# Hybrid encoder step on one core: order of the first loads, squares of the second tile on VectorE, order of the closings

## The reference, cut to what matters

```
h = x + W_out[concat(shortconv(xn), ssd(xn))],   xn = RMSNorm(x) * ln_mix_w,  xn @ W_in first
h = h + CrossAttn(RMSNorm(h), memory)            4 heads, 256 memory tokens
h = h + PEER(RMSNorm(h))                         8 heads x 16 experts per token out of 16384
y = RMSNorm(h) * final_norm_w
```

## Time and profile before

| | us |
|---|---|
| median of three runs | 1840.97 |
| their range | 1833.16 to 1843.06 |
| the profiled execution | 1838.45 |
| its span, first to last instruction | 1836.7 |
| TensorE, VectorE, GpSimd, ScalarE busy | 1689.9, 1225.0, 697.7, 369.2 |

### The profile page before, as it was taken

The page is one execution under the profiler, slowest core; times in us unless marked ns, Lnnn a source line. Parts: engine busy times, 40 slices in busy tenths (PEclk is TensorE's granted clock), DMA queues, the critical chain, the costliest instruction groups (busy, mean ns, idle before and its releaser), DMA issues. The chain is left out here.

```text
span 1836.7 us, 19834 instructions
## 1 busy us (share of the span) xinstructions
PE 1689.9 (92%) x7088; PEld 1256.1 (68%) x7088; DVE 1225.0 (67%) x2437; ACT 369.2 (20%) x912; POOL 697.7 (38%) x598
## 2 busy tenths in 40 slices
PE   6998999999777888898896999999999999999996
PEld 5887888877655677787785666666666666666542
DVE  1252111799688768898986999676656666656675
ACT  1031123111330244642660001101000000000101
POOL 0000000234124437731664555555444544534551
PEclk9999999999878999899898999999999999999998
DMA  5532444779336949995999999999999999999995
GB/s 168 180 110 99 153 138 138 240 249 349 101 134 204 379 167 367 338 329 184 361 346 415 409 409 410 409 407 410 406 409 410 397 410 409 396 409 405 377 409 221
DMA packets 238301, 563.10 MB, mean 307 GB/s; under 512 B 17068, under 2 KB 125276, under 8 KB 236156
## 3 DMA queue, kind: packets, MB, share of 16 engines
q0 software_dynamic: 82944, 302.03, 42.7%
q1 hardware_dynamic: 121512, 242.72, 36.1%
q10 hardware_dynamic: 33748, 17.10, 3.1%
HBM read 539.46 MB, written 21.66 MB: 306 GB/s over the span
## 5 line engine op out<-in xcount | busy, mean ns | idle before, releaser
L782 POOL DMA_INDIRECT M<-in_u_tab,IDX x288 | 331.3, 1150 | 736.5 <-DVE PEER L1742 358.0
L789 POOL DMA_INDIRECT M<-in_v_tab,IDX x288 | 362.8, 1260 | 369.2 <-DVE X L1763 299.3
L1093 PE MATMUL PSB<-XN,M 128*128 128x256 f32 x2048 | 469.0, 384 | 12.2 <-ACT M L1303 6.0
L1101 PE MATMUL PSB<-M,HST 128*128 128x512 f32 x1024 | 461.3, 596 | 10.4 <-DVE HST L1819 9.6
L1093 PEld LDWEIGHTS PSB<-XN,M 128*128 128x128 f32 x2048 | 393.5, 193 | 112.8 <-issue 53.2
L1742 DVE CUSTOM_DVE_ANT_0 M<-M,XN 128x1024 f32<-128x1024 f32 x288 | 351.8, 1223 | 146.7 <-DMA M<-in_u_tab,IDX 135.3
L1763 DVE SCALAR_TENSOR_TENSOR X<-M,PEER,X 128x1024 f32<-128x1024 f32 x256 | 328.1, 1282 | 101.4 <-DMA M<-in_v_tab,IDX 88.0
L831 PE MATMUL PSB<-M 128*128 128x256 f32 (+1 forms) x1408 | 333.4, 398 | 10.2 <-DVE M L1399 8.9
L1101 PEld LDWEIGHTS PSB<-M,HST 128*128 128x128 f32 x1024 | 194.8, 191 | 215.1 <-issue 198.5
L831 PEld LDWEIGHTS PSB<-M 128*128 128x128 f32 x1408 | 270.1, 193 | 66.4 <-DVE M L1399 9.8
L838 PE MATMUL PSB<-M 128*128 128x256 f32 (+1 forms) x1056 | 247.7, 395 | 2.5 <-DVE M L1399 1.6
(11 more groups left out here) (214 smaller groups left out, 1072.7 us busy)
## 6 DMA issues: line engine op xcount, KB each, us to landing
M<-in_u_blocks SPq DMA_DIRECT2D x128, 512.0 KB
M<-in_v_tab SPq DMA_DIRECT2D x128, 512.0 KB
M<-in_w_in SPq DMA_DIRECT2D x24, 1024.0 KB
M<-in_w_pq SPq DMA_DIRECT2D x16, 1024.0 KB
gate_spill<-M ACTq DMA_DIRECT2D x16, 1024.0 KB, 14.5
M<-gate_spill SPq DMA_DIRECT2D x16, 1024.0 KB, 11.1
M<-in_w_out SPq DMA_DIRECT2D x8, 1024.0 KB
M<-in_w_mq SPq DMA_DIRECT2D x8, 1024.0 KB
```

The costliest lines, as they stand in the source:

```text
L782: pool.indirect_dma_start(out=UA[:, s % RR, :], out_offset=None, in_=utab, in_offset=bass.IndirectOffsetOnAxis(ap=IDX[:, n:n + 1], axis=0) ...
L789: pool.indirect_dma_start(out=VA[:, s % RR, :], out_offset=None, in_=vtab, in_offset=bass.IndirectOffsetOnAxis(ap=IDX[:, n:n + 1], axis=0) ...
L1093: last = pe.matmul(PSB[:, 4 + b % 2, 0:2 * P], UBLK[:, b % SR, c, :], XN[:, 1:3, c * P:(c + 1) * P], start=(c == 0), stop=(c == DC - 1))
L1101: last = pe.matmul(PSB[:, 2 * t + hf, :], WR[:, b % WRING, t * P:(t + 1) * P], VBLK[:, b % SR, hf * 512:(hf + 1) * 512], start=(b == 0), s ...
```

## The change

At the start, SP loads tile 0, tile 1 and five of the nine small tables, and only then weight block 0, block 1, the state and block 2; ScalarE issues the other four small loads. VectorE sums the squares of tile 1 (`sq`), and ScalarE only takes the root of it; the list begins with `sq` of tile 1, `norm` of tile 0, `const`, `norm` of tile 1, and both turns. At the end, `fold` stands ahead of the last block's `vd`; then come both closings, the three roots in the order sample, tile 1, tile 2, and the three final scalings in that order. Closing tile 1 waits for the half of the last block that belongs to it.

```diff
+CLOSED = [4, 1, 2]
+SMALL_ROWS = [("ln_mix_w", ...), ("mem_norm_w", ...), ("ln_mem_w", ...), ("ssd_norm_w", ...), ("conv_a_w", ...),
+              ("conv_s_w", ...), ("conv_s_b", ...), ("cache_conv_a", ...), ("cache_conv_ssd", ...)]
@@ dense
     if g == 0:
-        s += [("const",)]
-        for t in TG[0]:
-            s += [("norm", 0, t), ("turn", 0, t)]
+        s += [("sq", 1), ("norm", 0, 0), ("const",), ("norm", 0, 1), ("turn", 0, 0), ("turn", 0, 1)]
@@ plan
+        if b == NBLK - 1:
+            out.append(("fold",))
         out.append(("vd", b))
...
-    for t in DENSE:
-        out += [("close", t), ("leave", t), ("final", t)]
-    return out + [("fold",), ("leave", NP), ("final", NP)]
+    out += [("close", t) for t in DENSE] + [("leave", t) for t in CLOSED]
+    return out + [("final", t) for t in CLOSED]
@@ SP
             sp.dma_start(X[:, 0, :], xp[0]).then_inc(x_in[0], 16)
+            sp.dma_start(X[:, 1, :], xp[1]).then_inc(x_in[1], 16)
+            for row in SMALL_ROWS[4:]:
+                load_small(sp, *row)
             load_block(sp, 0)
-            sp.dma_start(X[:, 1, :], xp[1]).then_inc(x_in[1], 16)
             load_block(sp, 1)
+            sp.dma_start(S0[:, :, :], a["state_ssd"]...).then_inc(state_in, 16)
             load_block(sp, 2)
@@ TensorE, vd
+                    if b == NBLK - 1 and t == 0:
+                        last.then_inc(first_closed, 1)
@@ ScalarE, norm
+                if (ph, t) == (0, 1):
+                    act.wait_ge(sq_done, 1)
+                    col = ROOTS.index(("norm", 0, 1))
+                    act.activation(SS[:, col:col + 1], SS[:, col:col + 1], ACT.Sqrt, bias=EPSC[:, :], scale=1.0 / D).then_inc(root_done, 1)
+                    return
@@ ScalarE, leave
-                if t in DENSE:
-                    act.wait_ge(closed, DENSE.index(t) + 1)
-                elif t < NP:
+                if t in CLOSED:
+                    act.wait_ge(closed, CLOSED.index(t) + 1)
+                else:
                     act.wait_ge(v_added, (step_of(t, PH - 1) + 1) * TOPK)
-                else:
-                    act.wait_ge(closed, 3)
@@ ScalarE, start
-            for name, r, pat in (... nine tables ...):
-                src = a[name].rearrange(pat, p=P)
-                act.dma_start(SMR[r:r + src.shape[0], :], src).then_inc(small_in, 16)
-            act.dma_start(S0[:, :, :], a["state_ssd"]...).then_inc(state_in, 16)
+            for row in SMALL_ROWS[:4]:
+                load_small(act, *row)
@@ VectorE
+            def sq(t):
+                col = ROOTS.index(("norm", 0, t))
+                dve.wait_ge(const_ok, 1)
+                dve.wait_ge(x_in[t], 16)
+                dve.tensor_tensor_reduce(XN[:, t, :], X[:, t, :], X[:, t, :], 1.0, 0.0, ALU.mult, ALU.add, SS[:, col:col + 1]).then_inc(sq_done, 1)
@@ VectorE, close
-                dve.wait_ge(vd_done, NBLK)
+                if t == DENSE[0]:
+                    dve.wait_ge(first_closed, 1)
+                else:
+                    dve.wait_ge(vd_done, NBLK)
```

More of the change, by code:

```diff
@@ L49 @@
 DENSE = [1, 2]
+CLOSED = [4, 1, 2]
+SMALL_ROWS = [("ln_mix_w", SM_MIX, "l (c p) -> (l c) p"), ("mem_norm_w", SM_MEMN, "l (c p) -> (l c) p"),
+              ("ln_mem_w", SM_LMEM, "l (c p) -> (l c) p"), ("ssd_norm_w", SM_SSD, "l (c p) -> (l c) p"),
+              ("conv_a_w", SM_CA, "l k (c p) -> (l k c) p"), ("conv_s_w", SM_CS, "l k (c p) -> (l k c) p"),
+              ("conv_s_b", SM_CB, "l (c p) -> (l c) p"), ("cache_conv_a", SM_HA, "l b k (c p) -> (l b k c) p"),
+              ("cache_conv_ssd", SM_HS, "l b k (c p) -> (l b k c) p")]
 def rows(t):
@@ L549, in build_program @@
         act_step, dve_step = sem("act_step"), sem("dve_step")
-        root_done = sem("root_done")
+        root_done, sq_done = sem("root_done"), sem("sq_done")
         xs_done = sem("xs_done")
@@ L567, in build_program @@
         gs_out, gr_in = [sem(f"gs_out{r}") for r in range(3)], [sem(f"gr_in{r}") for r in range(GRING)]
-        y_norm, y_out = sem("y_norm"), sem("y_out")
+        y_norm, y_out, first_closed = sem("y_norm"), sem("y_out"), sem("first_closed")
         def loc(t, gap=0):
@@ L618, in score_at, with load_small @@
             return [GAIN[:, 0:512], GAIN[:, 512:1024], EARLY[:, 0:512], EARLY[:, 512:1024]][b]
+        def load_small(eng, name, r, pat):
+            src = a[name].rearrange(pat, p=P)
+            eng.dma_start(SMR[r:r + src.shape[0], :], src).then_inc(small_in, 16)
         def load_block(sp, i):
@@ L632, in _ @@
             sp.dma_start(X[:, 0, :], xp[0]).then_inc(x_in[0], 16)
+            sp.dma_start(X[:, 1, :], xp[1]).then_inc(x_in[1], 16)
+            for row in SMALL_ROWS[4:]:
+                load_small(sp, *row)
             load_block(sp, 0)
-            sp.dma_start(X[:, 1, :], xp[1]).then_inc(x_in[1], 16)
             load_block(sp, 1)
+            sp.dma_start(S0[:, :, :], a["state_ssd"].rearrange("l b (x h) p n -> (h p) (l b x) n", h=2)).then_inc(state_in, 16)
             load_block(sp, 2)
@@ L1346, in leave @@
                 n = rows(t)
-                if t in DENSE:
-                    act.wait_ge(closed, DENSE.index(t) + 1)
-                elif t < NP:
+                if t in CLOSED:
+                    act.wait_ge(closed, CLOSED.index(t) + 1)
+                else:
                     act.wait_ge(v_added, (step_of(t, PH - 1) + 1) * TOPK)
-                else:
-                    act.wait_ge(closed, 3)
                 root_mean_square(("leave", t), XN[0:n, t, :], X[0:n, t, :], n, D)
[L1355 to L1359, removed]
-                src = a[name].rearrange(pat, p=P)
-                act.dma_start(SMR[r:r + src.shape[0], :], src).then_inc(small_in, 16)
-            act.dma_start(S0[:, :, :], a["state_ssd"].rearrange("l b (x h) p n -> (h p) (l b x) n", h=2)).then_inc(state_in, 16)
+            for row in SMALL_ROWS[:4]:
+                load_small(act, *row)
             act.wait_ge(const_ok, 1)
@@ L1833, in final @@
                 dve.scalar_tensor_tensor(out=x, in0=x, scalar=rs, in1=GAIN[0:n, :], op0=ALU.mult, op1=ALU.mult).then_inc(y_norm, 1)
-            does = {"const": const, "state": state, "norm": norm, "turn": turn, "memn": memn, "in": in_, "keep": keep, "ca": ca, "cs": cs, "dt": dt, "oc": oc,
+            does = {"sq": sq, "const": const, "state": state, "norm": norm, "turn": turn, "memn": memn, "in": in_, "keep": keep, "ca": ca, "cs": cs, "dt": dt, "oc": oc,
                     "kt": kt, "s1": s1, "s2": s2, "s3": s3, "s4": s4, "o": residual("o"), "a1": a1, "mo": residual("mo"),
```

## The result

The changed kernel takes 1821.8 us (median of 4 runs, 1818.53 to 1828.5) against 1841.04 (median of 4, 1833.16 to 1843.06). The ratio is 0.9911, 95% interval 0.9888 to 0.9935, which is 12 to 20.6 us less. I had said 1830.5 us and 10.5 us less, with a range down to 1825.5.

A forecast was written before the change was run, and what follows sets the result against it. It took the body as dense TensorE work, then saturated DMA transfer, with serial chains at both ends. Gains of 4.7 us at the start and 5.85 at the tail, 10.5 off 1840.97, gave 1830.5 us, range 1825.5 to 1838.

The forecast's parts named there:

- the size of the start: Before the first projection: starting at 13.3 instead of 18.03 us gains 4.7 us, with bounds of 2.0 and 5.8.
- tile 1's landing: Start loads: tile 1, issued second at about 1.27 us, lands at 6.4 us, with bounds 5.3 and 9.1.
- my second estimate: Tile 1's landing from the byte count plus the 1.1 to 1.4 us by which landings trail their bytes: 6.5 us.
- the first job: First sixteen matmuls of the projection: expected to take about 6.1 us again, as in the kernel before.
- TensorE reaches its full clock sooner: Rival at the first projection: nearly gapless transposes lift the clock, gaining up to 2.7 us more, 1827.8 us; chance 0.10.
- The tail: End of the kernel: fold before the last block and interleaved closings gain 5.85 us, with bounds 2.9 and 7.4.
- table load: ScalarE's activation table load in the closings: counted at 1.28 us, without the skill's 1.38 us drain.
- The larger last output: At the very end, a 512 KB tile goes out last instead of the 128 KB sample, giving back 0.65 us.
- The fold's wait: Before the last block: the last gather addition ends 3.0 us ahead of the fold, so TensorE waits for nothing.
- Start is lost on the way: Rival in the body: it absorbs what the start saves, leaving only the tail's gain, 1835.1 us; chance 0.16.
- slower, by the clock in the middle: Rival between 400 and 1000 us: 39 us more at half clock cost 19.5 us, giving 1850 us; chance 0.05.
- VectorE's squares cost nothing: Start: tile 0's scaling, queued behind tile 1's squares, goes at 7.8 instead of 6.3 us, without cost to the projection.

The follow-up runs named there:

- the change again: The changed kernel unaltered, run a second time in more rounds beside its halves; ratio 0.9924 to the kernel before.
- e6: Changed kernel with all nine small loads issued from ScalarE's queue; one run, within 1826.2 to 1829.8 us for four such kernels, beside 1841.2 before.
- e8: Changed kernel with tile 1's closing waiting for the whole last block; one run, within 1826.2 to 1829.8 us for four such kernels, beside 1841.2 before.
- the delayed one: Changed kernel with five idle repetitions of VectorE's sum of squares, 6.1 us, ahead of the real one; ratio 0.9952 to the kernel before.
- e12: Changed kernel without VectorE's squares, Sqrt table loaded before the fold, sample's last scaling on GpSimd, tile 2 scaled and sent in halves; ratio 0.9931 to before.
- third profile: Profile from the third set of runs of the unaltered changed kernel; that set's ratio was 0.9922 to the kernel before.
- start alone: Kernel before with only the change's start: loads, squares of tile 1 on VectorE, order of first steps; ratio 0.9952 to the kernel before.
- e5: Changed kernel with ScalarE squaring tile 1 instead of VectorE; one run, within 1826.2 to 1829.8 us for four such kernels, beside 1841.2 before.
- e7: Changed kernel with early fold but closings one after another, waiting for the whole block; one run, within 1826.2 to 1829.8 us for four such kernels.

## Why the prediction was wrong, and where it held

**What failed: the size of the start.** I had the projection start at 13.3 and gain 4.7 us; it starts at 12.47 and gains 5.6 by this row, 5.9 by the second copy, 6.7 in the mean of the profiles. Two terms of the sum were off. First, tile 1's landing, taken at 6.4, is 5.8 in the trace. The step from tile 0 to tile 1 was right: 1.35 us (4.41 to 5.76), where 524 KB at 385 GB/s had given 1.36. What was off was its start, since tile 0 itself lands at 0.81 + 3.6 = 4.41 and not at the 4.81 of the kernel before, and my second estimate: by the byte count and the lag it was 6.5, and I leaned towards it. From the landing to the projection it took 6.7 us, as against 6.9 in my sum. Second, I counted the first job at its old 6.1 us. It had a rival of its own, *TensorE reaches its full clock sooner*, at 0.10. Ten profiles have the new load order and no extra matmuls. In five the first job takes 3.75 us (the change again, e6, e8, the delayed one, e12), in the other five 5.5 to 5.8 (the change and its third profile, start alone, e5, e7); the three with the old start take 6.2 to 6.7. So it is worth 2.1 us in half of the profiles. The change alone shows both (5.84, 3.75, 5.70): I had treated as one case what is drawn anew in every execution, and it belonged in the sum with about half its size.

**The sum.** 6.7 at the start, 6.1 at the tail and 0.5 in the middle (1794.5 to 1794.0) make 13.3 us, and the runs give 14.4, give or take 1.1. What is between them is inside the error of either. The landmarks show no surplus in the middle beyond the 0.5, the granted clock of the runs hints at one of some 3 us, and this stays open. One sum of the tail was rounded up: 14.30 us over 34 matmuls is 0.42 each and not 0.43, which moves nothing by more than 0.1 us.

**The range.** The forecast was 8.7 us above the first median, 1830.5 to 1821.8. Of these, 3.9 us are gain that the sum lacked (10.5 against 14.4), of which the two terms of the start explain about 2; 1.7 are the base, 1840.97, which was high for a kernel whose 68 runs have a mean of 1839.3; and 3.1 are the luck of the first four runs, whose median lies below the mean of 1824.9. The lower end of the range, 1825.5, was 15.5 us under my base, and the first medians lie 19.2 apart. The error I gave the forecast, "about 2 us", was too small for a sum whose start alone had bounds of 2.0 to 5.8, and the real start (5.9 by the second copy, 6.7 with the clock) lies at or past the upper one. The median of all 16 runs, 1825.1, is just past the end of the range as well.

**What held.** The tail: forecast 5.85, measured 6.1, with all steps as said (sample's square while the last block runs, table load hidden, VectorE's scalings in a row, last scaling 7.2 us behind the half block against my 7.5). The larger last output gives back 0.7 as put: 3.1 us from the last scaling to the end of the span, against 2.4. The fold's wait had 3.1 us of slack, my 3.0. A lead is not lost in the body: the start alone gives 7.9 us, and the middle lasts 1791.7 to 1797.1 us whatever stands ahead of it. That it passes exactly one for one is inside the error, and no more than that. *Start is lost on the way* and *slower, by the clock in the middle* did not occur. That VectorE's squares cost nothing was wrong by 0.5 us: I saw that they stand in front of tile 0's scaling, but took both tiles as needed at once, while TensorE turns tile 0 first and is busy from then on to the projection.

**The transposes and the clock.** In five of ten profiles the level rose within or right behind sixteen transposes with no other matmul since the launch but the table's own transpose: 273 ns is the shortest of them in the second profile of the change. In the three with the old start, where they come as eight and eight with a wait of 1.6 us between, it did not. The Trainium skill (TensorE: Matmul & The Clock Gate, Part 4: PE-mode transpose) says that transposes don't count as busy for the clock; by that the rival was worth nothing. The measurement decides against the sentence for these float32 transposes. The table load takes 1.28 us in the change as it did before, with no drain behind it: 1817.03 to the root at 1818.32.

## What to carry to other kernels

Put first in a queue what the first dependent step needs, and weights, which are needed several microseconds later, behind it. Small tables that an early step waits for belong ahead of the weights too; with all nine on ScalarE's queue and the weights issued beside them they came 2.3 us later. At the end, an epilogue of independent tiles is a pipeline over engines, so write all additions, then all roots, then all scalings, and start with the tile whose input is ready. Before a rival is given a chance of its own, ask whether it is one case or a draw in each execution; a draw belongs in the sum.

## What the runs showed that I had not expected

- The same small loads are complete at 7.26 us from two queues and at 9.60 from ScalarE's alone, though the nine issues end at 3.6 and at about 4.4 us. In the second case the weight blocks are issued beside them.
- The granted clock of this kernel's middle differs between executions at the same instruction: eight transposes behind a wait of 2.62 us take 1.09 or 1.97 us. The clock column reads 1.00 in the first 28 us also where matmuls take 796 ns.
- With GpSimd at work on 32 rows, VectorE's scaling of 128x1024 takes 2.00 us instead of 1.28, and GpSimd itself takes 2.85 and 2.33 us for 32x1024. This is one profile.
